# Moving the shared expert's down products, parking three of them, and reordering the last sums of a one-core MoE decoder layer

## What is computed

```python
def moe_tokens(h, p):
    ...
    _, eidx = lax.top_k(jnp.where(emask, sel, -jnp.inf), TOP_K)      # 8 of 64 experts
    ...
    hg = jnp.einsum('td,edf->tef', h, p['w1'])
    hu = jnp.einsum('td,edf->tef', h, p['w3'])
    act = jax.nn.silu(hg) * hu * gate[:, :, None].astype(h.dtype)
    routed = jnp.einsum('tef,efd->td', act, p['w2'])
    shared = (jax.nn.silu(h @ p['ws1']) * (h @ p['ws3'])) @ p['ws2']
    return routed + shared

# in layer():
    f = lax.map(lambda hs: moe_tokens(hs, p), h)
    x = x + gt2 * rmsnorm(f, p['g_post2'])
```

## Time and profile before

| | us |
|---|---|
| median of 3 runs (1246.65 to 1248.0) | 1247.88 |
| the profiled execution's own time | 1246.15 |
| its span, from first to last recorded instruction | 1244.2 |
| PE busy | 1157.4 (93%) |
| DVE, POOL, ACT busy | 560.7, 524.7, 327.3 |

### The profile page before, as it was taken

How to read it: one execution, slowest core, us unless ns; L and a number is a source line. 1 busy time by engine, 2 the same in 40 slices (tenths; PEclk the granted TensorE clock), 3 DMA queues, 4 the chain that set the end, 5 groups by cost and what they waited for, 6 DMA issues and landing times.

```text
span 1244.2 us, 26196 instructions
## 1 busy us (share of the span) xinstructions
PE 1157.4 (93%) x9253; PEld 852.7 (69%) x9254; DVE 560.7 (45%) x912; ACT 327.3 (26%) x620; POOL 524.7 (42%) x527
## 2 busy tenths in 40 slices
PE   4899999999999899978899999978999997999897
PEld 3699999999999899966755555544455554555452
DVE  3285677659568868227743322211112221222134
ACT  3523322322333451335211221111111211111122
POOL 2144444445448244310665554452345444344420
PEclk9899999999999999998999999999999999999999
DMA  9954344424421232438789999999999999999987
GB/s 310 322 171 153 93 144 152 152 84 152 152 84 34 68 101 85 136 128 310 285 304 389 406 404 408 408 409 415 411 409 409 408 400 400 407 401 401 353 314 276
DMA packets 157224, 337.44 MB, mean 271 GB/s; under 512 B 14807, under 2 KB 99363, under 8 KB 139753
## 3 DMA queue, kind: packets, MB, share of 16 engines
q1 hardware_dynamic: 137496, 296.57, 64.2%
q0 software_dynamic: 16656, 34.14, 7.3%
q10 hardware_dynamic: 3025, 6.07, 1.4%
HBM read 322.21 MB, written 33.30 MB: 286 GB/s over the span
## 4 chain that ended last, share of the span: by engine, by line
PE 58%; SPq 20%; DMA 7%; issue 6%; DVE 6%; POOL 2%; ACT 1%; DVEq 0%; POOLq 0%; ACTq 0%
PE ps L1746 14%; SPq L356 12%; PE ps L1509 10%; PE ps L1510 9%; PE ps L1511 9%; PE ps L1760 6%; SPq L361 6%; DMA w<-in_w_dram 4%; DMA ring<-in_w_ada_dram 2%; PE ps L1522 1%; PE ps L1852 1%; SPq L388 1%; PE ps L1451 1%; PE ps L1754 1%; PE ps L1819 1%
## 5 line engine op out<-in xcount | busy, mean ns | idle before, releaser
L1746 PE MATMUL ps<-w,xe 128*64 x3136 | 367.2, 388 | 37.9 <-DMA w<-in_w_dram 32.1
L1746 PEld LDWEIGHTS ps<-w,xe 128*64 128x64 f32 x3136 | 229.6, 140 | 171.8 <-issue 77.5
L534 POOL TENSOR_TENSOR wsplit<-ring,wsplit 128x1024 fp32r<-128x1024 f32 x80 | 194.8, 2435 | 282.3 <-ACT wsplit L687 250.8
L1509 PE MATMUL ps<-h_s_hi,wsplit 128*128 128x260 f32 x960 | 272.4, 284 | 0.0
L1511 PE MATMUL ps<-h_s_hi,wsplit 128*128 128x260 f32 x960 | 270.8, 282 | 0.0
L1510 PE MATMUL ps<-h_lo_m_hi,wsplit 128*128 128x260 f32 x832 | 234.8, 282 | 0.0
L1371 DVE TENSOR_TENSOR rs<-sg,ps 128x128 f32<-128x128 f32 x98 | 28.2, 287 | 375.9 <-ACT sg L985 375.9
L1760 PE MATMUL ps<-w,eactT 128*64 (+1 forms) x784 | 185.2, 593 | 0.9 <-issue 0.8
L1509 PEld LDWEIGHTS ps<-h_s_hi,wsplit 128*128 128x128 f32 x960 | 180.6, 188 | 6.9 <-issue 5.9
L1511 PEld LDWEIGHTS ps<-h_s_hi,wsplit 128*128 128x128 f32 x960 | 180.8, 188 | 0.0
L687 ACT ACTIVATE wsplit<-ring 128x1024 fp32r<-128x1024 f32 x80 | 84.8, 1060 | 298.3 <-PE ps L1511 288.0
(11 more groups left out here) (333 smaller groups left out, 1344.1 us busy)
## 6 DMA issues: line engine op xcount, KB each, us to landing
w<-in_w_dram SPq DMA_DIRECT2D x192, 1024.0 KB, 20.8
ring<-in_w_in_dram SPq DMA_DIRECT2D x56, 512.0 KB, 3.7
ring<-in_w_ada_dram SPq DMA_DIRECT2D x8, 2048.0 KB, 8.7
ring<-in_w_ada_dram SPq DMA_DIRECT2D x8, 1024.0 KB, 21.9
ring<-y_rows SPq DMA_DIRECT2D x4, 2048.0 KB, 17.9
ring<-in_w_out_a_dram SPq DMA_DIRECT2D x8, 512.0 KB, 4.1
ring<-in_w_out_b_dram SPq DMA_DIRECT2D x8, 512.0 KB, 4.1
ring<-in_w_o_dram SPq DMA_DIRECT2D x8, 512.0 KB, 4.1
```

The costliest lines, as they stand in the source:

```text
L534: pool.tensor_tensor(wsplit[:, b, 1], raw[raw_slot], wsplit[:, b, 0], ALU.subtract).then_inc(S["w_lo"], 1)
L1509: mm(ps[:, bank + h, 0:HT], wsplit[:, b, 0, k, :], hi[:, k, p:q], start=(k == 0), stop=False)
L1746: ins = mm(ps[a * STRIP:(a + 1) * STRIP, 2 + f, 0:2 * P], xe[:, k, a * STRIP:(a + 1) * STRIP], w[a][:, k, :, f * P:(f + 1) * P], start=(k ...
```

## The change

1. The down products of all five tiles of the shared expert are made in pass 19, in `expert`'s pass body behind `pe.If(p == SHARED_AT)`. Tiles 2, 3 and the sample tile go by banks 6, 0 and 6 and are copied by ACT to SBUF (`park`, three copies of 1024 columns); tiles 1 and 0 stay in banks 0 and 6. The branch and the products stand in each of the 16 bodies of `expert` in PE's program.
2. Behind the last pass `unpark(n)` puts a parked tile back into PSUM: 2 matmuls with the identity in place of the 4 of `shared_down`.
3. The sample tile is finished ahead of tile 3 (`order`, `bank_of`, SP's and PE's order).
4. The late rows of tiles 0 and 1 are read in two steps of two choices each (`choice_rows`): choices 2 and 3 at two new marks (`rows_there(1 + TT)`, `rows_there(2 + TT)`; by the routing they are there after passes 44 and 45), choices 0 and 1 where the whole was read. A step is two transfers of 512 KB.
5. The shared weights are started by ACT at the head of pass 10 instead of by SP after 24 experts. The early half of tile 0 and the late half of tile 3 go to four pieces of SBUF instead of two (`split`), because some of the old place now holds the parked tiles.

```diff
-        split = [(xflat[:, 0:3 * D], 3), (slot_part(5, YF + D, D), 1)]
+        split = [(hflat[:, 0:D], 1), (xflat[:, 3 * D:4 * D], 1), (sflat[:, 2 * T:2 * T + D], 1), (slot_part(5, YF + D, D), 1)]
+        parked = [xflat[:, 0:D], xflat[:, D:2 * D], xflat[0:NS, 2 * D:3 * D]]
-        order = tuple(range(TT))
+        order = (0, 1, 2, TT - 1, TT - 2)
-        bank_of = (6, 0, 2, 4, 6)
+        bank_of = (6, 0, 2, 6, 4)
+        WS2_AT, SHARED_AT = TT, 19
@@ SP
-            with sp.Fori(1, 4) as g:
-                ...
-            sp.wait_ge(S["late_chain"], LA * TT)
-            for k in range(FT):
-                sp.dma_start(ws2_in[k], ws2[0, k * P:(k + 1) * P, :]).then_inc(w_late, 16)
-            with sp.Fori(4, E // DEEP) as g:
+            with sp.Fori(1, E // DEEP) as g:
             rows_there(0)
+            sp.wait_ge(S["sh_mm"], 2 * FT + TT)
             ...
-            rows_there(1)
-            tile_rows(y_last, 0, 0, y_last_in[0])
+            def choice_rows(i, choices):
+                part, at = y_last[i][0][0], i * P * TOPK
+                for k in choices:
+                    sp.dma_start(part[k::TOPK // 2].rearrange("t (b d) -> t b d", b=4),
+                                 y_rows[at:at + P * TOPK // 2, :].rearrange("(b t k) d -> k t b d", b=4, k=TOPK // 2)[k]
+                                 ).then_inc(y_last_in[i], 16)
+            rows_there(1 + TT)
+            choice_rows(0, (2, 3))
             slot_free(E - 2)
             sp.dma_start(G2s, g2_rows[1:NSEQ, :]).then_inc(g2_in, 16)
+            rows_there(2 + TT)
+            choice_rows(1, (2, 3))
+            rows_there(1)
+            choice_rows(0, (0, 1))
             rows_there(2)
-            tile_rows(y_last, 1, 0, y_last_in[1])
+            choice_rows(1, (0, 1))
             rows_there(3)
             slot_free(E - 1)
             tile_rows(y_last, 2, 0, y_last_in[2])
+            rows_there(TT)
+            sp.dma_start(ysmp, y_rows[NP * TOPK:T * TOPK, :]).then_inc(smp_in, 16)
             rows_there(4)
             sp.wait_ge(S["early_pe"], 1)
             tile_rows(y_last, 3, 0, y_last_in[3])
-            rows_there(TT)
-            sp.dma_start(ysmp, y_rows[NP * TOPK:T * TOPK, :]).then_inc(smp_in, 16)
@@ ACT
+            def park(n):
+                act.wait_ge(S["sh_mm"], 2 * FT + n + 1)
+                bank = (6, 0, 6)[n]
+                src = ps[0:NS if n == 2 else P, bank:bank + 2, :]
+                act.activation(parked[n], src.rearrange("p b n -> p (b n)"), ACT.Copy).then_inc(S["sh_ev"], 1)
             with act.Fori(0, pairs) as it:
                 for u in range(2):
+                    if u == 0:
+                        with act.If(it == WS2_AT):
+                            act.wait_ge(S["late_chain"], LA * TT)
+                            for k in range(FT):
+                                act.dma_start(ws2_in[k], ws2[0, k * P:(k + 1) * P, :]).then_inc(w_late, 16)
+                    else:
+                        with act.If(it == SHARED_AT // 2):
+                            for n in range(3):
+                                park(n)
                     one_pass(it * 2 + u, u)
@@ PE
+            def unpark(n):
+                bank, rows = (2, 4, 6)[n], (P, P, NS)[n]
+                for h in range(2):
+                    mm(ps[0:rows, bank + h, :], ident[0:rows, 0:rows], parked[n][:, h * 512:(h + 1) * 512], start=True, stop=False)
+            def shared_downs():
+                pe.wait_ge(w_late, 16 * C + 64)
+                shared_down(2, 6)
+                shared_down(3, 0)
+                pe.wait_ge(S["sh_ev"], 2 * FT + 1)
+                shared_down(TT - 1, 6)
+                pe.wait_ge(S["sh_ev"], 2 * FT + 2)
+                shared_down(1, 0)
+                pe.wait_ge(S["sh_ev"], 2 * FT + 3)
+                shared_down(0, 6)
             ...
+                        with pe.If(p == SHARED_AT):
+                            shared_downs()
                         pe.wait_ge(S["xe_dve"], p * 2 + 1)
             ...
-            pe.wait_ge(w_late, 16 * C + 64)
-            shared_down(0)
-            shared_down(1)
             ...
             pe.wait_ge(S["gm_dve"], 2)
-            shared_down(2)
             mark(gated_rows(0, 1, y_first), "early_pe")
             gated_rows(1, 1, y_first)
             pe.wait_ge(S["xe_dve"], passes * 2 + 2)
             last_sums(0)
+            unpark(0)
             pe.wait_ge(S["ex_yd"], passes + 2)
-            shared_down(3)
+            unpark(1)
             last_sums(1)
             gated_rows(2, 1, y_first)
+            gated_rows(4, 1, y_first)
             last_sums(2)
-            gated_rows(3, 1, y_first)
             pe.wait_ge(S["yacc"], 1)
-            shared_down(TT - 1)
-            last_sums(TT - 2)
+            unpark(2)
             pe.wait_ge(smp_in, 16)
             for c in range(2):
                 ins = mm(ps[0:NS, bank_of[3] + c, :], gmat_s, ...)
             mark(ins, "stat_mm")
+            last_sums(4)
```

More of the change, by code:

```diff
@@ L208, in build_program @@
         xgs = [sflat[:, 0:D], conv[:, 0:D]]
+        split = [(hflat[:, 0:D], 1), (xflat[:, 3 * D:4 * D], 1), (sflat[:, 2 * T:2 * T + D], 1), (slot_part(5, YF + D, D), 1)]
+        y_first = [split] + [whole(t) for t in (slot_part(5, 0, YF), slot_part(0, 0, YF), slot_part(1, 0, YF))]
+        y_last = [whole(t) for t in (slot_part(2, 0, YF), slot_part(3, 0, YF), slot_part(4, 0, YF))] + [split]
+        parked = [xflat[:, 0:D], xflat[:, D:2 * D], xflat[0:NS, 2 * D:3 * D]]
         esil, eact = sg[:, 0:256], rs[:, 0:256]
@@ L1282, in _ @@
             link(dve.tensor_copy(last_of[:, 1:1 + TT], val8[:, :, 0]), wait=False)
+            link(dve.tensor_copy(last_of[:, 1 + TT:MARKS], val8[:, 0:EARLY, 2]), wait=False)
             link(dve.tensor_reduce(first_strip, below, AX.X, ALU.add))
@@ L1314, in _ @@
             link(tt(first_at, beyond, one64[0:1, :], ALU.add), "table_dve")
-            link(dve.tensor_reduce(red[0:1 + TT, 2:3], ps[0:1 + TT, 6, 0:P], AX.X, ALU.max), "early_dve", wait=False)
+            link(dve.tensor_reduce(red[0:MARKS, 2:3], ps[0:MARKS, 6, 0:P], AX.X, ALU.max), "early_dve", wait=False)
             tile_no = dve.alloc_register("tile_no")
@@ L1354, in _ @@
             dve.wait_ge(S["es_pe"], 2)
-            last_pass = few[:, 4:5 + TT]
-            link(ts(last_pass, ps[0:1, 6, P:P + 1 + TT], 4.0 * P - 1.0, None, ALU.add), "early_dve")
+            last_pass = few[:, 4:4 + MARKS]
+            link(ts(last_pass, ps[0:1, 6, P:P + MARKS], 4.0 * P - 1.0, None, ALU.add), "early_dve")
             link(ts(last_pass, last_pass, 7, None, ALU.logical_shift_right), "last_pass_dve", wait=False)
@@ L1726, in _ @@
             pe.wait_ge(S["es_dve"], 1)
-            mm(ps[0:1 + TT, 6, 0:P], last_of, ident[:, :], start=True, stop=True)
+            mm(ps[0:MARKS, 6, 0:P], last_of, ident[:, :], start=True, stop=True)
             mm(ps[0:1, 6, 3 * P:4 * P], red[:, 0:1], ident[:, :], start=True, stop=True).then_inc(S["es_pe"], 1)
@@ L1764, in _ @@
             pe.wait_ge(S["early_dve"], 1)
-            mm(ps[0:1, 6, P:P + 1 + TT], red[0:1 + TT, 2:3], ident[0:1 + TT, 0:1 + TT], start=True, stop=True).then_inc(S["es_pe"], 1)
+            mm(ps[0:1, 6, P:P + MARKS], red[0:MARKS, 2:3], ident[0:MARKS, 0:MARKS], start=True, stop=True).then_inc(S["es_pe"], 1)
             at_step = pe.alloc_register("step_pe")
@@ L1775, in _, with shared_down @@
             pe.wait_ge(S["early_dve"], 2)
+            def shared_down(i, f):
+                rows = P if i < TT - 1 else LAST
+                for h in range(2):
+                    for k in range(FT):
+                        ins = mm(ps[0:rows, f + h, :], scr[:, 2 + k, i * P:i * P + rows], ws2_in[k][:, h * 512:(h + 1) * 512],
+                                 start=(k == 0), stop=(k == FT - 1 and i > 1))
+                ins.then_inc(S["sh_mm"], 1)
+            def unpark(n):
+                bank, rows = (2, 4, 6)[n], (P, P, NS)[n]
+                for h in range(2):
+                    mm(ps[0:rows, bank + h, :], ident[0:rows, 0:rows], parked[n][:, h * 512:(h + 1) * 512], start=True, stop=False)
[9 more added lines that the diff above has]
+                shared_down(0, 6)
             def expert(e, u, turn):
@@ L1811, in expert @@
                         down_product(down, 1, 1).then_inc(S["ex_y"], 1)
[L1813 to L1817, removed]
-                    for k in range(FT):
-                        mm(ps[0:rows, f + h, :], scr[:, 2 + k, i * P:i * P + rows], ws2_in[k][:, h * 512:(h + 1) * 512],
-                           start=(k == 0), stop=False)
             with pe.Fori(0, 5) as g:
@@ L1847, in gated_rows @@
                 i, f = order[n], bank_of[n]
+                blocks = [part[:, a * D:(a + 1) * D] for part, n_ in src[i] for a in range(n_)]
                 for c in range(2):
                     for b in range(4):
-                        part, n = src[i][0] if b < src[i][0][1] else src[i][1]
```

(9 more changed lines are left out.)

10 lines of the change are left out of this document (4 added, 6 removed).

## The result

The changed kernel takes 1397.87 us (median of 4 runs, 1392.95 to 1399.21), the kernel before beside it 1247.94 us: a ratio of 1.1201, 95% interval 1.1185 to 1.1217. It is 12% slower; the prediction was 1246.7 us, with a range up to 1251.5. The profiled execution took 1392.95 us with a span of 1391.2 us.

The account below looks back on a forecast made before the run. Full DMA engines and the weight stream were taken to set the pace, then PE and row reads together in the tail. Nothing before 1209.9 and 1.2 us off the tail gave 1246.7 us against 1247.88; range 1243.6 to 1251.5.

Parts of the forecast that it names:

- Rival B: Expert loops: PE's longer loop, about 7 blocks a round, no longer stays on the chip; 1251 us, chance 0.20.
- 60 fetches on full DMA engines: Later expert rounds: some 60 fetches at 1.07 us cost 4 us spread over all engines, up to 47 on one.
- Pass 19 and what hides it: Pass 19: five down products add 20 us, hidden by PE's later waits; cost 0, bounds 0 to 2 us.
- The branch and the weights by ACT at nothing: Every pass's comparison: 0, at most 0.1 us in each of four; weights started by ACT in pass 10: 0.
- The wait ahead of tile 0's late sum: Tail: tile 0's second step lands at 1216.9, PE wants it at 1213.7; a new wait of about 3 us.
- The tail's gain: After the last pass: PE has 5.5 us less work, the end comes 1.0 us earlier, taken as 1.2 us.
- rival C: Tail gets no shorter: longer wait at tile 0 or delayed tile 3 rows, last write 1245.3; 1249 us, chance 0.10.
- Rival A: Tail row reads: lagging DMA engines don't matter, PE isn't held at tile 0; 1244.6 us, chance 0.22.

Follow-up runs that it names:

- e2_one_body: The changed kernel with the five shared products only in the one expert body that runs pass 19 on these inputs: 1247.78 us, ratio 1.0011 to the kernel before.
- e12_parking_alone: The changed kernel with the products in one body, late rows read whole and tile 3 ahead of the sample tile: 1246.70 us, ratio 1.0000 to the kernel before.
- e5_unrun10: The kernel before with 10 never executed matmuls behind a comparison in each of the 16 expert bodies: 1250.26 us, ratio 1.0019.
- (18, 32): The kernel before with 18 never executed matmuls in each expert body and 32 ahead of the loops: 1412.34 us, ratio 1.1333.
- e7_small_early: The changed kernel with products in one body and the sample tile's put-back moved ahead of two half sums: 1248.48 us, ratio 1.0010 to the kernel before.

## Why the prediction was wrong, point by point

**The rival that came true was priced at 3 us and cost 150.** Rival B named the mechanism (PE's expert loop isn't kept on the chip, some 7 blocks a round) and its sign in the profile (q8 packets in later rounds); both came out. It was given 0.20 and 1251 us. Three terms of it failed. First the count of stalls: it counted the rounds, 8, while the jump over an expert without a pass leaves the sequence as well; 20 gaps instead of 8. The sentence behind that was "17 experts without a pass are jumped over between passes already, ... so a jump is covered by matmuls in the queue": true in the kernel before, whose loops fetch nothing after their first round. Second the price: "a few us of PE that the waits absorb" were 5.8 us for a jump back, some 5 for a jump over, 13.1 for both together, plus some 2 us of half clock in the pass behind each. Third the absorption: the waits for weights were 32 us, and they did vanish, but the gaps came to 153.6 us (17.6 of them the products of pass 19, nearly all of the rest waiting) and the passes took 29.9 us more. With the 2 us of half clock behind each, 32 us have room for two double jumps or four single ones. The cost that the prediction worked out with most care, 60 fetches on full DMA engines, is not what took the time: the engines were less busy than before.

**The chance.** The prediction's own count gave 7 blocks where 6 were the longest loop seen to be kept, and "no run here shows the limit". For an unknown limit between 6 and something, with 80 instructions added to each of a loop's six bodies, 0.20 was low; the runs put the limit at 6.0 to 6.4 blocks, by place.

**Pass 19 and what hides it: right, but for one step.** In `e2_one_body` the chain runs

```profile
837.63 19.93 PE ps L1810 x40
857.56 6.20 PE ps L1774 x56
```

against 837.7 to 857.6 forecast. The prediction lets pass 21 end at 890.2 and yet calls pass 22, which started at 889.2, "no later than before"; its own sum made it 1 us later, and it started at 891.4, 2.2 us later. The next wait for weights took that up: pass 24 starts at 915.3 against 915.5, pass 45 at 1164.3 (forecast 1164.6). The waits for weights went from 32.1 to 24.1 us, 6.9 of them ahead of the products: the rest was the cover. In the changed kernel itself pass 19 lay behind stalls of its own.

**The branch and the weights by ACT at nothing: right,** as far as these runs tell. `e12_parking_alone` has the weights by ACT and stands at 1.0000; its comparison stands in one body only. `e5_unrun10` has a comparison in every body, and its passes take 11.0 us where they don't follow a wait, as before. Its median is 2.4 us higher (1.0019, 1.0008 to 1.0031), with 35.0 us of waits for weights instead of 32.1; whether the comparison or the longer loop makes these wasn't tried.

**The wait ahead of tile 0's late sum: right.** Forecast: rows at 1216.9 and a new wait of about 3 us; `e2_one_body` started the sum at 1216.66, after a wait of 2.2 us.

**The tail's gain: wrong in the size of PE's pieces.** From 1216.66 PE took 21.3 us instead of 17.9. The sum of tile 0 took 2.80 instead of 1.76 and the two put-backs behind it 4.40 instead of 3.66, at the lower clock behind the new wait (the prediction had applied exactly this to pass 19 and forgotten it here); the last half tile took 3.44 instead of 1.76, behind the small matmuls and at 0.53 of the clock. Together 3.5 us. So tile 3's rows, there at 1233.6, didn't set the end, PE did (1237.9), and the tail of that kernel was no shorter than before, 34.8 us against 34.3; rival C, with its last write at 1245.3, is what it came to, for another reason. In the changed kernel the tail was 1.0 us shorter, as forecast, but that is luck, since its chain is another one: PE waited for tile 3's rows

```profile
1370.40 9.65 DMA act<-y_rows
1380.05 0.04 issue
1380.09 3.69 PE ps L1896 x16
```

and summed at the half clock.

**Rival A (the laggards don't matter)** fell with the landing at 1216.5 in `e2_one_body`.

## What to carry to other kernels

Count the instructions of a loop before adding to its body: each added matmul counts once per unrolled body, executed or not, and a loop on PE that grows past some 6 blocks of 256 (about 380 fp32 matmuls; here 6.0 blocks were kept and of 6.4 only some) can pay 5 us and more at its jumps, so rare code belongs in one body or outside of the loop. The sign is in the profile's page: q8 packets beyond the first round, and idle time of PE with "issue" as its releaser at jumps only. When a rival names an unknown limit that the change may cross, price it by the number of all jumps and against the sum of the waits that are to absorb it, not by a round figure.

## What the runs showed of the hardware that I had not expected

- A jump to instructions that aren't on the chip cost PE 4.5 to 6 us in the changed kernel, and two jumps close together 12.4 to 14.0 us, though one packet of 16 KB takes 1.07 us of a DMA engine. These are no fixed prices: with 14 matmuls that never run, a double jump took up to 18.4 us, and with (18, 32) a jump back up to 11.4. What fills the rest isn't shown. Straight code costs nothing: 26 of 48 passes follow without a gap while blocks are fetched.
- Whether a loop is kept depends on where it lies: 25 matmuls ahead of it, never executed, swapped which of two equal loops of 6.4 blocks was kept. It isn't the place alone, since single rounds of dropped loops had no fetch.
- TensorE's granted clock fell to 0.53 without a wait, behind 3.6 us of matmuls with left sides of 8 by 8 and 64 by 8 (`e2_one_body`); with the two apart it stayed at 1.00 (`e7_small_early`, 1234.8 to 1236.7 us), and so it did behind 3.6 us of 128 by 8 (before, 1233.0 to 1234.8 us).
- At the end DVE is a bound too: 2.64 us per tile, whatever its rows (8 or 128), as soon as three tiles come together.
